# Low parts of the gated units placed 32, 96 or 64 bytes further on, by stage

## The reference, cut to what matters

```python
# block 1, after its mixer: ffn0
ff = silu(h @ w_gate) * (h @ w_up)          # 1024 -> 2816
x = x + ff @ w_down                         # 2816 -> 1024
# block 2, 16 meta tokens put ahead (1040 tokens): ffn1, mixer, ffn2
h = h + 0.5 * swiglu(rmsnorm(h, ffn1_norm), ffn1_w1, ffn1_w3, ffn1_w2)
...
h = h + 0.5 * swiglu(rmsnorm(h, ffn2_norm), ffn2_w1, ffn2_w3, ffn2_w2)
```

## Time and profile before

| | |
|---|---|
| median of three runs | 3608.77 us |
| the profiled execution's own time | 3607.34 us |
| its span, first to last instruction | 3605.6 us |
| mean granted clock of TensorE | 0.991 |
| PE busy | 3520.8 us (98%) |
| VectorE, ScalarE, GpSimd busy | 41%, 27%, 31% |
| triples with `ff` as moving operand | 880 of 512 columns, 352 of 264 |
| triples with `h` as moving operand at L731 to L733 | 2688 of 512 columns, 832 of 264 |

### The profile page before, as it was taken

One profiled execution on the slowest core, in us unless ns is written; L12 is line 12 of the kernel. 1 busy time (PEld: TensorE's weight loads), 2 busy tenths in 40 slices (PEclk: granted clock), 3 DMA queues, 4 the chain that ended last, 5 costly groups with the idle time before them and its releaser, 6 DMA issues.

```text
span 3605.6 us, 52857 instructions
## 1 busy us (share of the span) xinstructions
PE 3520.8 (98%) x20076; PEld 2933.4 (81%) x20076; DVE 1465.4 (41%) x2553; ACT 963.0 (27%) x1684; POOL 1132.6 (31%) x1499
## 2 busy tenths in 40 slices
PE   8999899999999999999999999999999999999998
PEld 6787778888888889899999878887777888888886
DVE  7865545211111263322122563737876521111214
ACT  5254533111111142110111332215663411111112
POOL 4433045222223252222222532300025532222323
PEclk9999899999999999999999999999999999999999
DMA  3113022111111121111111332110024311111113
GB/s 125 41 49 86 1 100 82 51 54 42 51 40 54 48 81 49 46 47 47 47 47 45 99 101 69 42 35 33 33 92 149 94 57 54 47 44 50 47 45 102
DMA packets 81556, 218.51 MB, mean 61 GB/s; under 512 B 18928, under 2 KB 19056, under 8 KB 80880
## 3 DMA queue, kind: packets, MB, share of 16 engines
q1 hardware_dynamic: 61792, 173.35, 15.5%
q10 hardware_dynamic: 19600, 42.88, 3.3%
HBM read 195.67 MB, written 19.46 MB: 60 GB/s over the span
## 4 chain that ended last, share of the span: by engine, by line
issue 61%; POOL 24%; PE 9%; DVE 4%; ACT 1%; POOLq 1%; DMA 0%; DVEq 0%; ACTq 0%; SPq 0%
POOL w_lo L572 24%; PE acc L731 2%; PE acc L732 2%; PE acc L733 2%; DVE cv_acc L1747 2%; PE acc L1281 0%; PE acc L1276 0%; POOLq L576 0%; PE acc L1398 0%; DVE ssq L680 0%; PE acc L1340 0%; PE acc L1415 0%; DVE tmp L692 0%; DVE cvo L1838 0%; PE acc L1407 0%
## 5 line engine op out<-in xcount | busy, mean ns | idle before, releaser
L572 POOL TENSOR_TENSOR w_lo<-w_raw,w_hi 128x256 fp32r<-128x256 f32 (+3 forms) x1480 | 1111.8, 782 | 2352.4 <-ACT w_hi L542 2351.9
L731 PE MATMUL acc<-h_hi,w_hi 128*128 128x512 f32 (+1 forms) x3520 | 1301.4, 370 | 15.8 <-issue 4.7
L732 PE MATMUL acc<-h_lo,w_hi 128*128 128x512 f32 (+1 forms) x3520 | 1300.8, 370 | 0.0
L733 PE MATMUL acc<-h_hi,w_lo 128*128 128x512 f32 (+1 forms) x3520 | 1295.7, 368 | 0.0
L731 PEld LDWEIGHTS acc<-h_hi,w_hi 128*128 128x128 f32 x3520 | 662.7, 188 | 143.2 <-issue 13.3
L732 PEld LDWEIGHTS acc<-h_lo,w_hi 128*128 128x128 f32 x3520 | 662.0, 188 | 118.3 <-issue 1.9
L733 PEld LDWEIGHTS acc<-h_hi,w_lo 128*128 128x128 f32 x3520 | 663.3, 188 | 114.9
L542 ACT CAST w_hi<-w_raw 128x1024 fp32r<-128x1024 f32 (+3 forms) x370 | 346.3, 936 | 1205.1 <-PE acc L733 1190.5
L1012 DVE TENSOR_TENSOR ff_hi<-tmp,acc 128x512 f32 (+3 forms) x154 | 94.6, 614 | 1098.6 <-PE acc L733 1066.6
L731 PE MATMUL acc<-ff_hi,w_hi 128*128 128x512 f32 (+1 forms) x1232 | 447.2, 363 | 6.1 <-POOL w_lo L572 3.4
L732 PE MATMUL acc<-ff_lo,w_hi 128*128 128x512 f32 (+1 forms) x1232 | 443.2, 360 | 0.0
(11 more groups left out here) (377 smaller groups left out, 3010.4 us busy)
## 6 DMA issues: line engine op xcount, KB each, us to landing
w_raw<-in_ffn_w_dram SPq DMA_DIRECT2D x94, 512.0 KB, 3.5
w_raw<-in_w_in_dram SPq DMA_DIRECT2D x60, 512.0 KB, 3.5
w_raw<-in_w_out_dram SPq DMA_DIRECT2D x32, 512.0 KB, 3.5
w_raw<-in_ffn_w_dram SPq DMA_DIRECT2D x48, 320.0 KB, 2.8
w_raw<-in_w_gate_dram SPq DMA_DIRECT2D x24, 512.0 KB, 3.5
w_raw<-in_w_up_dram SPq DMA_DIRECT2D x24, 512.0 KB, 3.5
w_raw<-in_ffn_w_dram SPq DMA_DIRECT2D x32, 384.0 KB, 3.0
gates_kept<-gstage ACTq DMA_DIRECT2D x32, 256.0 KB, 2.0
```

The costliest lines, as they stand in the source:

```text
L572: pool.tensor_tensor(w_lo[:, j, a:a + step], w_raw[:, j, a:a + step], w_hi[:, j, a:a + step].bitcast(F32), ALU.subtract).then_inc(split_do ...
L731: pe.matmul(bank, wh, rh, start=(k == 0), stop=False)
L732: pe.matmul(bank, wh, rl, start=False, stop=False)
L733: ins = pe.matmul(bank, wl, rh, start=False, stop=(k == seg.kt - 1))
```

## The change

Until now one pair of tensors, `ff_hi` and `ff_lo`, served all three stages. Now each stage has its own pair over the same memory. The high parts stay where they were; the low parts begin 32 bytes further on in ffn0, 96 in ffn1 and 64 in ffn2. What lies behind them (`tmp`, `ssq`, `rs`, `sq`, `ahead_u`, and `ahead2` inside the free row) moves by 96 bytes to make room. Weights, `h`, chunks, waits and the order of instructions on every engine are the same.

```diff
+LOW_SHIFT = dict(ffn0=32, ffn1=96, ffn2=64)
...
-        behind = ff_at[1] + FMAX * 4 * ROW
+        behind = ff_at[1] + FMAX * 4 * ROW + 96
         x = place("x", W, [P, KD, L])
-        ff_hi = place("ff_hi", W + ff_at[0], [P, FMAX, ROW], F32R)
-        ff_lo = place("ff_lo", W + ff_at[1], [P, FMAX, ROW], F32R)
+        ff_of = {name: (place(f"{name}_hi", W + ff_at[0], [P, FMAX, ROW], F32R),
+                        place(f"{name}_lo", W + ff_at[1] + LOW_SHIFT[name], [P, FMAX, ROW], F32R))
+                 for name in ("ffn0", "ffn1", "ffn2")}
...
-                 place("ahead2", free_row[1], [P, 512])]
+                 place("ahead2", free_row[1] + 96, [P, 512])]
...
-                    pe_slab(pe, down, 0, 0, (ff_hi, ff_lo), only=c)
-                pe_slab(pe, down, 0, 1, (ff_hi, ff_lo))
+                    pe_slab(pe, down, 0, 0, ff_of[name], only=c)
+                pe_slab(pe, down, 0, 1, ff_of[name])
...
         def dve_ffn(dve, own, name, chunks, scale, beside):
 
             n = len(chunks)
+            ff_hi, ff_lo = ff_of[name]
```

More of the change, by code:

```diff
@@ L939, in pe_ffn @@
                 if part == len(FQ) - 1:
-                    pe_last(pe, then, (SEG[f"{name}_down{part}a"], SEG[f"{name}_down{part}b"]), (ff_hi, ff_lo), name)
+                    pe_last(pe, then, (SEG[f"{name}_down{part}a"], SEG[f"{name}_down{part}b"]), ff_of[name], name)
                     break
@@ L944, in pe_ffn @@
                     pe.wait_ge(sem("ff_" + name), part * len(chunks) + c + 1)
-                    pe_slab(pe, down, 0, 0, (ff_hi, ff_lo), only=c)
-                pe_slab(pe, down, 0, 1, (ff_hi, ff_lo))
+                    pe_slab(pe, down, 0, 0, ff_of[name], only=c)
+                pe_slab(pe, down, 0, 1, ff_of[name])
                 with pe.Fori(1, down.pairs) as i:
                     for j in range(2):
-                        pe_slab(pe, down, i, j, (ff_hi, ff_lo))
+                        pe_slab(pe, down, i, j, ff_of[name])
         def early_of(name):
```

## The result

The changed kernel takes 3623.06 us in the median of seven runs (3619.23 to 3623.68), against 3609.23 for the kernel before in seven: 1.0038 times, 95% interval 1.0027 to 1.005. The profiled execution has a span of 3621.3 us against 3605.6. It is slower by 14 us; 3622 was forecast.

The account below looks back on a forecast made before the run. PE, busy 98%, bounds the kernel: matmul count times distance between starts. The profiled 3607.34 us plus 13.5 gave 3620.8, or 3622.3 by the median; 3622 was forecast, range 3596 to 3640 us.

Parts of the forecast that it names:

- items 1 and 3: Downs: L732's moved streams cost 13.5 us; L731 and L733 read unmoved data, their changed neighbour already counted in that price.
- The nearest row: Streams of `h`, one phase change per triple: 13.8 ns per triple of 512 columns, 12.1 us over 880 triples.
- isolated changes: Phase steps in a down slab of ffn1: each costs some 10 ns, a constant phase nothing; 17.6 us over 880 triples.
- item 1: L732 reading shifted low parts in the downs: each triple leaves its phase and returns, 13.5 us, upper bound 27.0 us.
- case C: Rival for the downs: only L732's shifted stream pays 4.6 ns more, 4.5 us in all, 3612 us; chance 0.10.
- 880 triples: Triples of 512 columns in the downs: 352 in ffn0, 352 in ffn2, 176 in ffn1's third chunk; 12.1 us at `h`'s price.
- B: Rival for the downs: every phase step paid in full, both directions, 27.0 us, 3634 us; chance 0.17.
- E: Rival for the downs: another phase lets memory accesses miss each other, gaining 9.0 us or more, 3598 us; chance 0.17.
- D: Rival for the downs: address has no part, something unseen sets `h` apart, no change, 3607 us; chance 0.14.
- Item 2: L1017's low-part writes and moved scratch on VectorE and ScalarE: 2 us at most either way, taken as 0, hidden behind PE.

## Why the prediction was right, and where it was not

**The time and its place.** 3622 was forecast and 3623.06 measured. The loss is in the downs, 13.7 us of span against 13.5 in the sum; the ups and the waits stood still, as items 1 and 3 said. The nearest row, `h`, gave the right size, by a wrong account of what makes `h` slow.

**The step that failed** in the mechanism is the sentence "It is the step that costs, not the place", in the isolated changes of item 1. With both parts moved no stream steps, and the price is at its highest, 19.9 ns. What counts is whether stream and weights begin at one phase modulo 256: with a match, at 128 or at 192, 65.3 us; without one, 65.9 to 67.2. `hx` and `ff` had the match, at 128 against 128; I had put down their speed to a phase that stays. The case C was turned away by ffn1's chunks at 64 and 96, and those have 264 columns, for which 64 and 32 behind cost nothing. It was a row of another length, used for a question in which length decides.

**Why the size came out all the same.** `h` costs more than `ff` because three of its four phases miss the weights, not because it steps. Three quarters of the 19.9 ns of a miss is 14.9, and the whole up of 576 matmuls gives 15.1 (133.46 us); the prediction's rows gave 13.8, to the rounding of the starts. Tile by tile it is less neat: a matching tile of `h` takes 690 ns, not 680, between neighbours that miss. That the changed kernel, with one stream in three off, pays 19.9, 15.9 and 13 ns by stage, and so 13.7 us in all, near what `h` would pay, is partly luck: other shifts would have given another sum. In the second downs 96 or 128 bytes cost 13.2 ns, 192 only 6.8. I had also counted all 880 triples; the last half down of ffn0 (105 matmuls) took 28.67 us against 28.66. 35 triples at 19.9 ns would be 0.7 us. But at 226.7 ns its matmuls of before take 23.8 us, so 4.9 us are pauses, of which the profile puts 2.0 to `w_lo` from GpSimd; the longer matmuls went into these pauses.

**The rivals.** B (27 us) is gone with the step, and E (a gain) too: no shift gained. D is gone: a stream's cost hangs on where the weights lie, 65.29 or 67.20 us for the same work. The prediction had given this case to the Trainium skill. Its page "SBUF — State Buffer" (section "Who interferes with whom") does say that PE and ACT never wait on anyone, but in a section on engines that contend for shared ports. No run here shows PE held up by another engine's accesses, so the sentence stands; that an address is then worth nothing was the prediction's own conclusion, and it is the conclusion that fails. So was "whatever the address" beside the figure of 215.7 ns, where the page is silent on addresses. C comes nearest in its words (a pair of stream and weights at different phases), but not in its price: one stream off makes its neighbours slow too, so that the loss was 13.7 us and not 4.5. Only 64 bytes back costs one stream's share, 6.8 ns.

**Item 2** stands: the downs with the scratch alone moved are as before, and PE's wait for VectorE's residual is 2.5 us.

**What stays open** is the mechanism. That a load and a stream that run beside each other meet in the memory fits the period of 256 bytes and the effect of `w_lo` alone, but nothing here shows the memory, and no run separates a stream's own weights from those that are loaded beside it. Nor do the runs explain the order of the prices for the low part alone, why ffn0's first down and its second differ at the same addresses (66.02 and 67.20 us with the weights moved, 67.28 and 66.56 with the low part 128 further on), why 264 columns hardly care, or why the ups grew a little shorter with `w_lo` moved. Shifts under 32 bytes were not tried.

## What to carry to other kernels

Where a kernel is bound by TensorE, read the distance between starts in steady stretches and compare segments of the same shape: 231.7 against 226.7 ns in the streams of `h` was worth 27 us here, 0.8% of the kernel. Look then at the start addresses of the moving operand and of the weights, modulo 256 bytes; for the fp32r streams of 512 columns here only equal ones ran at 226.7 ns, and a row pitch of 4160 bytes, no multiple of 256, lost the match at three tiles of four. And size a cost by a row of the same shape: a row of 264 columns told the opposite of what 512 do.

## What the runs showed of the hardware that was not expected

- A matmul of 128x512 in fp32r, with its own load of 128x128 weights, starts every 226.7 ns (65.29 us for 288) when stream and weights begin at one phase modulo 256. With all streams off it starts every 233.3 ns (67.20 us) at most offsets, 232.4 at 128, and 229 in one down, at the full clock in all. The difference of 6.7 ns is, as an estimate, 16 cycles of 2.4 GHz. With one stream of three off, triples cost 6.8, 13.2 and 19.9 ns more, near one, two and three times that, but also 15.9 and 16.7.
- The same addresses can settle at two prices: 687 and 700 ns per triple in ffn0's first and second down with the weights moved by 192, 700 and 693 with the low part moved by 128. Once a down has settled, its price stays to its end, and the later downs of ffn0 keep the second one.
- For 264 columns the match counts for little: in ffn1's second downs a triple takes 360 to 367 ns at all offsets tried, and 360 also 64 bytes behind the weights.
- A shift of the low parts by 256 bytes left the second downs of ffn0 and ffn1 at 65.29 and 67.42 us, and 192 forward (6.8 ns) costs what 64 back does (6.9).
